# The last block's cross-attention in a hybrid decoder trunk: two chunks of scores standing at a time, memory keys and values fetched during w_out

## The reference, cut to what matters

```
z, xBC, dt, q, k, v = rmsnorm(h) @ w_in
h = h + concat(ssd(z, xBC, dt), window_attention(q, k, v)) @ w_out
h = h + cross_attention(rmsnorm(h), mem_k, mem_v) @ w_co
h = h + (silu(hn @ w_gate) * (hn @ w_up)) @ w_down        # hn = rmsnorm(h)
y = rmsnorm(h)
```

```
q = (hn @ w_cq).reshape(b, L, 4, 128)
s = einsum('blhd,bmhd->bhlm', q, mem_k) * 128 ** -0.5
p = softmax(s, axis=-1)
o = einsum('bhlm,bmhd->blhd', p, mem_v)
out = o.reshape(b, L, 512) @ w_co
```

## Time and profile before

| what | value |
| --- | --- |
| median of three runs | 3088.08 us (3085.93 to 3090.31) |
| the profiled execution | 3090.34 us |
| its span in the profile | 3088.6 us |
| TensorE matmul busy | 2898.3 us, 94% of the span |
| VectorE, ScalarE, GpSimd busy | 1473.0, 1152.9, 1000.9 us |
| mean granted TensorE clock, where 1 is full speed | 0.963 |

### The profile page before, as it was taken

One profiled execution on the slowest core, in us unless ns is written; L12 is line 12 of the kernel. 1 busy time (PEld: TensorE's weight loads), 2 busy tenths in 40 slices (PEclk: granted clock), 3 DMA queues, 4 the chain that ended last, 5 costly groups with the idle time before them and its releaser, 6 DMA issues.

```text
span 3088.6 us, 36148 instructions
## 1 busy us (share of the span) xinstructions
PE 2898.3 (94%) x14245; PEld 2348.4 (76%) x14245; DVE 1473.0 (48%) x2236; ACT 1152.9 (37%) x1861; POOL 1000.9 (32%) x451
## 2 busy tenths in 40 slices
PE   7868968999999999999999999999999968999998
PEld 3446856888877878878778778787788757888887
DVE  3244556555664256557662465566632524222214
ACT  2224544444354234543452345444532323121212
POOL 1112203333334433333334443333344312333331
PEclk9869978999999999999999999999999979999999
DMA  9352356322222345232223353322233421222221
GB/s 310 108 150 62 123 126 166 100 82 79 75 75 82 96 127 147 76 88 75 72 76 96 109 150 96 89 75 69 79 93 96 137 72 55 69 76 69 75 69 56
DMA packets 442041, 303.11 MB, mean 98 GB/s; under 512 B 47371, under 2 KB 416143, under 8 KB 440834
## 3 DMA queue, kind: packets, MB, share of 16 engines
q1 hardware_dynamic: 439418, 294.41, 32.5%
q10 hardware_dynamic: 1880, 6.34, 0.6%
q0 software_dynamic: 576, 0.07, 0.0%
HBM read 277.90 MB, written 23.85 MB: 98 GB/s over the span
## 4 chain that ended last, share of the span: by engine, by line
PE 78%; DVE 7%; DMA 3%; ACT 2%; issue 2%; DVEq 1%; SPq 1%; POOL 0%; ACTq 0%
PE L L2334 22%; PE L L2329 21%; PE L L2330 21%; PE G L2333 3%; DMA xin<-in_x_prompt_dram 1%; PE G L2485 1%; PE G L2458 1%; PE G L2473 1%; DVE sqsum L1849 1%; PE G L2429 1%; DMA xt<-xT_dram 1%; PE G L2524 1%; PE G L1299 0%; PE G L2503 0%; PE G L1294 0%
## 5 line engine op out<-in xcount | busy, mean ns | idle before, releaser
L1498 POOL TENSOR_TENSOR w_lo<-w_raw,w_hi 128x1024 fp32r<-128x1024 f32 x367 | 894.1, 2440 | 1713.9 <-ACT w_hi L1512 1713.9
L2334 PE MATMUL L<-xa_l,w_hi 128*128 128x512 f32 x1536 | 632.4, 412 | 0.0
L2329 PE MATMUL L<-xa_h,w_hi 128*128 128x512 f32 x1536 | 614.0, 400 | 3.1 <-DVE xa_l L2126 3.1
L2330 PE MATMUL L<-xa_h,w_lo 128*128 128x512 f32 x1536 | 604.0, 393 | 0.0
L1512 ACT ACTIVATE w_hi<-w_raw 128x1024 fp32r<-128x1024 f32 x367 | 386.4, 1054 | 378.4 <-PE L L2334 357.3
L2263 DVE TENSOR_TENSOR sg<-sg,L 128x512 f32<-128x512 f32 x88 | 60.5, 687 | 600.5 <-PE L L2334 600.5
L2329 PEld LDWEIGHTS L<-xa_h,w_hi 128*128 128x128 f32 x1536 | 292.4, 190 | 59.2 <-issue 11.4
L2330 PEld LDWEIGHTS L<-xa_h,w_lo 128*128 128x128 f32 x1536 | 290.8, 189 | 60.8 <-issue 1.0
L2334 PEld LDWEIGHTS L<-xa_l,w_hi 128*128 128x128 f32 x1536 | 291.8, 190 | 48.2
L2334 PE MATMUL L<-hid_l,w_hi 128*128 128x512 f32 x704 | 289.7, 412 | 0.0
L2329 PE MATMUL L<-hid_h,w_hi 128*128 128x512 f32 x704 | 279.9, 398 | 6.2 <-DVE hT L2275 6.2
(11 more groups left out here) (505 smaller groups left out, 4508.9 us busy)
## 6 DMA issues: line engine op xcount, KB each, us to landing
w_raw<-in_w_up_dram SPq DMA_DIRECT2D x82, 512.0 KB, 3.8
w_raw<-in_w_down_dram SPq DMA_DIRECT2D x77, 512.0 KB, 3.4
w_raw<-in_w_gate_dram SPq DMA_DIRECT2D x72, 512.0 KB, 3.8
w_raw<-in_w_in_dram SPq DMA_DIRECT2D x56, 512.0 KB, 3.9
xt<-xT_dram SPq DMA_DIRECT2D x56, 256.0 KB, 4.1
fwin<-in_w_in_dram SPq DMA_DIRECT2D x8, 1156.0 KB, 10.6
xin<-in_x_prompt_dram SPq DMA_DIRECT2D x16, 512.0 KB, 5.5
w_raw<-in_w_in_dram SPq DMA_DIRECT2D x32, 256.0 KB, 3.7
```

Of the source, the lines that this page charges most:

```text
L1498: pool.tensor_tensor(w_lo[:, n % RING, 0:w], raw_of(n)[:, 0:w], w_hi[:, n % RING, 0:w].bitcast(F32), ALU.subtract)\
L2329: pe.matmul(acc, wh, rh, start=(k == 0), stop=False)
L2330: pe.matmul(acc, wl, rh, start=False, stop=False)
L2334: last = pe.matmul(acc, wh, rl, start=False, stop=(k == kn - 1))
```

## The change

For the last block alone there is a function of its own, `last_cross`, on each of the three engines. The blocks 0 to 2 keep `cross`.

First, the keys and values of the last block get places of their own, `km3_h`, `km3_l` and `vm3`, on the memory of `xb_h`, which in the last block nothing writes. Their three fetches stand in ScalarE's program ahead of the squares of the fifth w_out panel.

Second, the scores of the chunks 0 and 2 go to `G`'s banks 0 and 1 and those of the chunks 1 and 3 to the two banks of `L`. TensorE computes the scores of two chunks at the start, and those of chunk c+2 right behind the transposes of chunk c.

```
+        km3_h = at("km3_h", O_B, [P, CH, NMEM], F32R)
+        km3_l = at("km3_l", O_B + 4096, [P, CH, NMEM], F32R)
+        vm3 = at("vm3", O_B + 8192, [P, 2, CH * P])
...
+            def last_scores(c, h):
+                return (G if c % 2 == 0 else L)[:, h // 2, (h % 2) * 256:(h % 2) * 256 + 256]
...  ScalarE
+                def last_cross():
+                    w0 = C * (NBLK - 1)
+                    def exps(c):
+                        act.wait_ge(s["xmax"], w0 + c + 1)
+                        if c >= 2:
+                            act.wait_ge(s["xpt"], w0 + c - 1)
+                        for h in range(CH):
+                            act.activation(PC[:, c % 2, h, :], last_scores(c, h), ACT.Exp, bias=cs_[:, c % 2, 0, h:h + 1],
+                                           accum_out=cs_[:, c % 2, 1, h:h + 1]).then_inc(s["xexp"], 1)
+                    exps(0)
+                    exps(1)
+                    for c in range(C):
+                        act.wait_ge(s["xpt"], w0 + c + 1)
+                        act.wait_ge(s["xo"], w0 + c - 1)
+                        act.activation(PTc[:, c % 2], G[:, 2:4, :].rearrange("p a (i t) -> p (a i) t", t=P), ACT.Copy)\
+                           .then_inc(s["xptsb"], 1)
+                        if c + 2 < C:
+                            exps(c + 2)
+                        act.wait_ge(s["xo"], w0 + c + 1)
+                        act.activation(cq_h[:, :, c * P:c * P + P], bank(4).rearrange("p (h t) -> p h t", t=P),
+                                       ACT.Copy).then_inc(s["o_hi"], 1)
...
+                        if not more and n == 4:
+                            act.wait_ge(s["lin_out"], out_of("W", b, 0) + 1)
+                            memory_in(km3_h, km3_l, vm3)
...
-                    act.wait_ge(s["lin_out"], out_of("Q", b, CH - 1) + 1)
-                    act.dma_start(km_h[:].bitcast(F32), kmh_dram.ap().rearrange("p (h m) -> p h m", h=CH)).then_inc(s["km_in"], 16)
-                    act.dma_start(km_l[:].bitcast(F32), kml_dram.ap().rearrange("p (h m) -> p h m", h=CH)).then_inc(s["km_in"], 16)
-                    act.dma_start(vm[:], vm_dram.ap().rearrange("p (c n) -> p c n", c=2)).then_inc(s["km_in"], 16)
-                    over = cross(b)
                     if more:
+                        act.wait_ge(s["lin_out"], out_of("Q", b, CH - 1) + 1)
+                        memory_in(km_h, km_l, vm)
+                        over = cross(b)
                         window(b + 1, WIN2, over)
-                    for _ in over:
-                        pass
+                        for _ in over:
+                            pass
+                    else:
+                        last_cross()
...  VectorE
+                    maxima(0)
+                    maxima(1)
+                    shares(0)
+                    shares(1)
+                    for c in range(C):
+                        if c + 2 < C:
+                            maxima(c + 2)
+                        dve.wait_ge(s["o_hi"], w0 + c + 1)
+                        cols = slice(c * P, c * P + P)
+                        dve.tensor_tensor(cq_l[:, :, cols], bank(4).rearrange("p (h t) -> p h t", t=P),
+                                          cq_h[:, :, cols].bitcast(F32), ALU.subtract).then_inc(s["o_lo"], 1)
+                        if c + 2 < C:
+                            shares(c + 2)
...  TensorE
+                    pe.wait_ge(s["cq_lo"], CH * NBLK)
+                    pe.wait_ge(s["km_in"], 48 * NBLK)
+                    scores(0)
+                    scores(1)
+                    for c in range(C):
+                        pe.wait_ge(s["xprob"], w0 + c + 1)
+                        pe.wait_ge(s["xptsb"], w0 + c)
+                        for i in range(2 * CH):
+                            last = pe.transpose(G[:, 2 + i // 4, (i % 4) * P:(i % 4) * P + P],
+                                                PC[:, c % 2, i // 2, (i % 2) * P:(i % 2) * P + P], ident[:])
+                        last.then_inc(s["xpt"], 1)
+                        if c + 2 < C:
+                            scores(c + 2)
+                        pe.wait_ge(s["xptsb"], w0 + c + 1)
+                        if c >= 1:
+                            pe.wait_ge(s["o_lo"], w0 + c)
+                        for h in range(CH):
+                            for m in range(2):
+                                last = pe.matmul(bank(4)[:, h * P:h * P + P], vm3[:, m, h * P:h * P + P],
+                                                 PTc[:, c % 2, 2 * h + m, :], start=(m == 0), stop=(m == 1))
+                        last.then_inc(s["xo"], 1)
```

More of the change, by code:

```diff
@@ L1688, in cross, with memory_in @@
                         yield
+                def memory_in(high, low, values_):
+                    act.dma_start(high[:].bitcast(F32), kmh_dram.ap().rearrange("p (h m) -> p h m", h=CH)).then_inc(s["km_in"], 16)
+                    act.dma_start(low[:].bitcast(F32), kml_dram.ap().rearrange("p (h m) -> p h m", h=CH)).then_inc(s["km_in"], 16)
+                    act.dma_start(values_[:], vm_dram.ap().rearrange("p (c n) -> p c n", c=2)).then_inc(s["km_in"], 16)
+                def last_cross():
[19 more added lines that the diff above has]
+                                       ACT.Copy).then_inc(s["o_hi"], 1)
                 def norm3_hi(b, i):
@@ L2116, in cross, with last_cross, maxima, shares @@
                         yield
+                def last_cross():
+                    w0 = C * (NBLK - 1)
+                    def maxima(c):
+                        dve.wait_ge(s["xs"], w0 + c + 1)
+                        src = G[:, 0:2, :] if c % 2 == 0 else L[:, 0:2, :]
+                        dve.tensor_reduce(cs_[:, c % 2, 0, :], src.rearrange("p a (h m) -> p (a h) m", h=2),
+                                          AX_X, ALU.max, negate=True).then_inc(s["xmax"], 1)
+                    def shares(c):
+                        dve.wait_ge(s["xexp"], CH * (w0 + c + 1))
+                        dve.reciprocal(cs_[:, c % 2, 2, :], cs_[:, c % 2, 1, :])
+                        dve.drain()
+                        dve.tensor_tensor(PC[:, c % 2], PC[:, c % 2],
+                                          cs_[:, c % 2, 2, :].unsqueeze(2).to_broadcast([P, CH, NMEM]), ALU.mult)\
+                           .then_inc(s["xprob"], 1)
+                    maxima(0)
[11 more added lines that the diff above has]
+                            shares(c + 2)
                 def norm3_t(b, i):
@@ L2527, in cross, with last_cross, scores @@
                         yield
+                def last_cross():
+                    w0 = C * (NBLK - 1)
+                    def scores(c):
+                        if c >= 2:
+                            pe.wait_ge(s["xexp"], CH * (w0 + c - 1))
+                        for h in range(CH):
+                            o = last_scores(c, h)
+                            qh, ql = cq_h[:, h, c * P:c * P + P], cq_l[:, h, c * P:c * P + P]
+                            pe.matmul(o, qh, km3_h[:, h, :], start=True, stop=False)
+                            pe.matmul(o, qh, km3_l[:, h, :], start=False, stop=False)
+                            last = pe.matmul(o, ql, km3_h[:, h, :], start=False, stop=True)
+                        last.then_inc(s["xs"], 1)
+                    pe.wait_ge(s["cq_lo"], CH * NBLK)
[14 more added lines that the diff above has]
+                            pe.wait_ge(s["o_lo"], w0 + c)
+                        for h in range(CH):
+                            for m in range(2):
+                                last = pe.matmul(bank(4)[:, h * P:h * P + P], vm3[:, m, h * P:h * P + P],
+                                                 PTc[:, c % 2, 2 * h + m, :], start=(m == 0), stop=(m == 1))
+                        last.then_inc(s["xo"], 1)
                 def last_rows(second):
```

## The result

The changed kernel took 3066.76 us (median of four runs, 3062.24 to 3071.04), the kernel before beside it 3089.19 us (median of four, 3085.93 to 3092.13). The ratio is 0.9932, with a 95% interval from 0.9917 to 0.9947, so 21 us faster, within 16 to 26. In five more runs the ratio was 0.9937 (0.9925 to 0.995). The forecast was 3072, in a range from 3066 to 3080.

A forecast was written before the change was run, and what follows sets the result against it. TensorE, busy 94% of the span, was taken as the bound, so only its idle or lower-clock time pays. Gains of 7.7 and 8.2 us, together 15.9, take the median of 3088.1 to 3072 us, range 3066 to 3080.

The forecast's parts named there:

- The fetches: Moved to the w_out stage: TensorE's wait ahead of the last scores shrinks, gain 7.7 us, price 0, 1 us at worst.
- the margin: W_out stage: the seventh panel's residual tile is hurt first by the moved transfers, with about 2 us to spare.
- The cross-attention: Last block, first score to first w_co matmul: 32.6 us in place of 40.8, gain 8.2 us, ends -0.4 and 13.2.
- All three parts of the walk: Last cross-attention: scores of chunk 2 end at 11.2 us, then 11.2 to values of chunk 2, then 10.2 to w_co.
- the list of signs: Last cross-attention: 24 score matmuls at about 0.115 us each, first transposes about 6.4 us after the first score.
- The ends of the range for the clock: Last cross-attention in the new order: 27.6 us all at full clock, 41.2 us all at the lower clock.
- The w_co stage unchanged: Behind the last cross-attention: no gain counted, its start at the lower clock left as before.
- The clock stays low: Rival, last cross-attention: TensorE at the lower clock throughout, 41.2 us, total 3080.8 us; chance 0.09.
- All at full clock: Rival, last cross-attention: TensorE at full clock throughout, 27.6 us, total 3067.2 us; chance 0.06.
- The order of VectorE gives the overlap back: Rival, last cross-attention: shares queued behind `cq_l` keep it at 40.8 us, 7.7 us won, total 3080.4 us; chance 0.08.
- Slower: Rival, w_out stage: the 1.5 MB delay a residual tile or panel and starve TensorE, 3088 us its edge; chance 0.03.
- The sum: Whole kernel: 7.7 us from the fetches plus 8.2 us from the cross-attention, 15.9 us in all.

The follow-up runs named there:

- the kernel with doubled fetches: Changed kernel plus the same three fetches of 512 KB once more into free memory, waited for by the scores too; ratio 0.9931 to the kernel before.
- kept busy: Changed kernel plus 60 matmuls whose result nobody reads, put in TensorE's waits in the last cross-attention; cross-attention 26.90 us, ratio 0.9916 to the kernel before.
- two chunks alone: Changed kernel with the three fetches put back behind the last w_cq matmul, new score order kept; cross-attention 29.61 us, ratio 0.9954 to the kernel before.
- the early fetch: Kernel before with only the three fetches moved to the w_out stage, cross-attention in its old order; cross-attention 37.55 us, ratio 0.9965 to the kernel before.

## Why the prediction was right, and where its sizes were off

**What bounds and where.** Right. TensorE's wait behind a transfer and the chain between engines in the last cross-attention were where the time was, and what was won in them reached the end, but for 0.2 us: TensorE is as busy in the feed-forward part as before.

**The fetches: 7.7 us, at no cost in the w_out stage.** Measured 7.7, with the releaser that was named. The cost in time was nil, and the price on the neighbours came out as forecast: the residual tiles took 8.9 us to land, where 4.1 + 4.4 had been allowed. But the picture of the new place was off in two ways. ScalarE's queue issued the fetches ahead of and alongside the rounding, with only the third in the idle time behind it, and needed 1.77 and 1.50 us for two of them. And what breaks first when the transfers double is a w_cq panel, and behind it VectorE's last addition beside GpSimd, not the residual tile on which I had put the margin.

**The cross-attention: 32.6 us forecast, 30.27 measured.** All three parts of the walk were too long, and in the first two errors partly cancel. I had both first scores at full clock and the first transposes 6.3 us after the start (6.4 in the list of signs). In the profiled execution the clock fell in the middle of these 24 matmuls:

```profile
2497.91 0.28 PE L2616 MATMUL G<-km_h,cq_h 128*128 128x256 f32 x1
...
2498.41 0.41 PE L2616 MATMUL L<-km_h,cq_h 128*128 128x256 f32 x1
```

So the second maximum began only at 2501.21, the first shares stood behind it, and the first transposes came 7.15 us after the start, 0.85 late. These transposes then ran at full clock (1.09 us) where I had put the lower, and the scores of chunk 2 ended 10.77 us after the start in place of 11.2. The picture that I had drawn, 24 matmuls at full clock and then the transposes at the lower one, did come in the kernel with doubled fetches (first transposes after 6.50 us, 1.97 us long), and its cross-attention took 30.48 us all the same. Where the clock falls differs from execution to execution, so that part of the forecast could only come true by luck. The chain of VectorE and ScalarE from there to the values of chunk 2 took 2507.50 to 2517.86, 10.36 us in place of 11.2: I had charged every step with a hand-over between engines, but instructions that follow each other on the same engine overlap by some 0.1 us. In the changed kernel the maximum begins before the shares have ended:

```profile
2512.08 1.23 DVE L2175 TENSOR_TENSOR PC<-PC,cs__111 128x1024 f32<-128x1024 f32 x1
2513.22 1.22 DVE L2168 TENSOR_REDUCE cs__111<-L 128x4 f32<-128x1024 f32 x1
```

And the end, from the values of chunk 2 to the w_co stage, took 9.14 us in place of 10.2: of the two values only one ran at the lower clock, and not to its end (3.17 us), and the other at full (2.05), where I had counted one and a half, at 1.84 extra each.

**The ends of the range for the clock.** I had worked out 27.6 us for the new order at full clock; kept busy, it took 26.90, so the walk was sound to 0.7 us. What I missed is that the old order has such an end too: it takes 34.14 us at full clock. Compared at the same clock the order gives 7.2 us, and the other 3.3 come from the clock. The prediction took them as one number.

**The w_co stage unchanged.** Right as to the change: in the second profile of the kernel before it takes 24.24 us too. But the start at the lower clock, which I had left in, belongs to the one execution that was profiled first, and in that pair of profiles the stage seemed to give 1.8 us.

**The rivals.** "The clock stays low" failed: it was 0.83 in the mean. Filled waits brought 3.4 us, so waits do cost clock here. The page that was named for this rival (the Trainium skill, "TensorE: Matmul & The Clock Gate", section "HAM oscillation — how this bites in real kernels") describes bursts behind waits for transfers, each of which starts cold. The trace agrees for TensorE's wait of 9.88 us (first score matmul 0.55 us). It does not extend to the waits for VectorE: in the kernel before, the clock stayed at 1.00 through two of 3.01 us (2517.3 to 2520.2 and 2534.3 to 2537.3), and both transposes behind them ran at full clock (1.10 us). "All at full clock" had 3067.2, and the median of 3066.76 lies nearest to it, but that is a coincidence of numbers: the clock was 0.83, and the cross-attention 2.7 us longer than the 27.6 of this rival. "The order of VectorE gives the overlap back" failed, in the changed kernel and in the one with two chunks alone. "Slower" was far off; with twice the transfers it cost 2.5 us.

**The sum.** 15.9 us forecast. The profiled pair gives 19.3; the 3.4 more are 2.3 of the cross-attention's terms, 1.8 of the w_co stage's clock, and -0.7 that lie outside the change. The medians gave 22.4 in the first comparison and 20.3 in the second. So the mechanism was right and the gain was 3 to 6 us larger than forecast, and 3066.76 us is inside the range of 3066 to 3080 by only 0.8 us: that it is inside is partly luck.

What is beyond the profiles lies in the spread of the runs. In the profiles the last w_cq matmul ended anywhere from 2481.0 to 2494.6 us, in kernels whose programs up to the w_out stage are the same. Most of that arises in the first block: the thousand matmul rows that take 254.9 us in the kernel before (376.2 to 631.1, mean clock 0.81 and then 0.95) take 245.0 in the kernel with two chunks alone (0.83 and then 1.00), and 6.9 of these 9.9 us are TensorE's own busy time. So a single whole run can be compared only to about 10 us. A stretch repeats better: two profiles of one kernel differ by 0.34 and 0.36 us in the cross-attention, but by 1.8 in the w_co stage when the clock falls in it. All stretches but these rest on one profile each.

## What to carry to other kernels

Compare two orders of a chain at the same clock: find what each takes with TensorE kept busy, and only then what the waits cost through the clock. A wait ahead of a burst is paid as idle time, and it can be paid again in the burst's lower clock: with the old order the early fetch was followed by a cross-attention 3.3 us shorter, with the new order by none. So gains of two edits that both shorten waits need not add. Where one stage stands alone and its engines hand work to each other, look first for what is fetched or computed inside it and could have been ready, then for a second set of banks. Before a step is moved ahead in one engine's queue, look at what then stands behind it: moving ScalarE's copy won 1.66 us for one chunk and cost 1.50 at the next.

## What the runs showed of the hardware that was not expected

A VectorE addition of two 128x512 operands from SBUF took 0.68 us alone and 2.82 us beside a GpSimd subtraction of 128x1024. One such addition took 2.68 us in the w_out stage of the kernel before and of the changed one too, beside the same work of GpSimd.

An issue of a 512 KB fetch on ScalarE's queue took 0.33 to 0.53 us in the old place and up to 1.77 us when SyncE's queue was issuing too. The first one was issued at 2445.17, before the engine began, at 2446.22, an instruction that stands earlier in its program.

The same program meets the lower clock at different places: after the same wait of 2.17 us behind w_cq it fell within the first 24 score matmuls in two profiles of the changed kernel, and in the kernel with doubled fetches not before the first transposes. The lengths of the cross-attention were 30.27, 30.63 and 30.48 us.
